# Prefix sums of a stick-breaking mixer in two rounded passes, value turns behind their slab, gate in PSUM, and fewer query columns

## What is computed

```python
z = einsum('bhqd,bhkd->bhqk', qb, kh) * scale
valid = key_pos < qpos
log_keep = where(valid, log_sigmoid(-z), 0.0)
after = cumsum(log_keep, axis=3, reverse=True) - log_keep
attn = where(valid, exp(log_sigmoid(z) + after), 0.0)      # then attn @ v, 8 heads of 64
u = a * sigmoid(b)                                         # GLU, then a causal conv of width 31 on 512 channels
```

## Time and profile before

| what | value |
|---|---|
| median of 3 runs | 1518.4 us (1518.07 to 1519.37) |
| profiled execution, its own time | 1519.34 us |
| its span in the profile | 1516.8 us |
| mean granted TensorE clock | 0.995 |
| PE busy | 1497.6 us (99%) |
| DVE busy | 1060.8 us (70%) |
| ACT busy | 757.5 us (50%) |
| POOL busy | 406.2 us (27%) |
| DMA | 250.90 MB, 165 GB/s mean |

### The profile page before, as it was taken

The page is one execution under the profiler, slowest core; times in us unless marked ns, Lnnn a source line. Parts: engine busy times, 40 slices in busy tenths (PEclk is TensorE's granted clock), DMA queues, the critical chain, the costliest instruction groups (busy, mean ns, idle before and its releaser), DMA issues.

```text
span 1516.8 us, 31248 instructions
## 1 busy us (share of the span) xinstructions
PE 1497.6 (99%) x11573; PEld 1447.4 (95%) x11573; DVE 1060.8 (70%) x1609; ACT 757.5 (50%) x1067; POOL 406.2 (27%) x162
## 2 busy tenths in 40 slices
PE   9999999999999999999999999999999999999997
PEld 7999999989999998999999999999998989999986
DVE  6438888758657778889765645755548998887854
ACT  6546655545444344457544544444444447644542
POOL 5542000533434300000244343434410000034452
PEclk9999999999999999999999999999999999999998
DMA  7334566655555544345555554556645335555662
GB/s 258 112 98 149 174 189 191 214 153 164 181 177 198 164 129 149 112 125 166 174 177 177 189 187 136 181 172 191 199 130 153 122 116 156 176 180 180 198 226 88
DMA packets 66119, 250.90 MB, mean 165 GB/s; under 512 B 7552, under 2 KB 8832, under 8 KB 66048
## 3 DMA queue, kind: packets, MB, share of 16 engines
q1 hardware_dynamic: 66048, 249.92, 52.6%
HBM read 248.84 MB, written 1.05 MB: 165 GB/s over the span
## 4 chain that ended last, share of the span: by engine, by line
PE 93%; DVE 5%; ACT 1%; issue 0%; DVEq 0%; ACTq 0%
PE W L1406 25%; PE W L1408 25%; PE W L1407 25%; PE W L1478 5%; PE XP L1502 4%; PE W L1477 3%; PE XQ L1502 2%; DVE scr L1265 2%; DVE wlo L825 1%; PE W L1446 1%; PE W L1447 1%; PE W L1448 1%; DVE proj L842 1%; PE XQ L1425 0%; ACT whi L428 0%
## 5 line engine op out<-in xcount | busy, mean ns | idle before, releaser
L1406 PE MATMUL W<-xh,whi 128*128 128x272 f32 (+2 forms) x2400 | 696.4, 290 | 1.6 <-DVE wlo L825 1.6
L381 POOL TENSOR_TENSOR wlo<-raw,whi 128x1024 fp32r<-128x1024 f32 (+1 forms) x151 | 403.6, 2674 | 1098.3 <-ACT whi L428 1098.3
L1408 PE MATMUL W<-xh,wlo 128*128 128x272 f32 (+2 forms) x2400 | 688.6, 287 | 0.0
L1407 PE MATMUL W<-xl,whi 128*128 128x272 f32 (+2 forms) x2400 | 686.8, 286 | 0.0
L428 ACT ACTIVATE whi<-raw 128x1024 fp32r<-128x1024 f32 (+1 forms) x437 | 482.0, 1109 | 143.6 <-PE W L1408 117.4
L1406 PEld LDWEIGHTS W<-xh,whi 128*128 128x128 f32 x2400 | 452.7, 189 | 7.1 <-issue 5.6
L1408 PEld LDWEIGHTS W<-xh,wlo 128*128 128x128 f32 x2400 | 453.0, 189 | 0.0
L1407 PEld LDWEIGHTS W<-xl,whi 128*128 128x128 f32 x2400 | 452.7, 189 | 0.3
L825 DVE TENSOR_TENSOR wlo<-raw,whi 128x1024 fp32r<-128x1024 f32 (+1 forms) x285 | 370.6, 1301 | 72.8 <-ACT whi L428 72.2
L1406 PE MATMUL W<-ax,whi 128*128 128x272 f32 (+2 forms) x816 | 235.1, 288 | 1.1 <-DVE ax L1239 0.5
L1408 PE MATMUL W<-ax,wlo 128*128 128x272 f32 (+2 forms) x816 | 234.3, 287 | 0.0
(11 more groups left out here) (235 smaller groups left out, 1202.4 us busy)
## 6 DMA issues: line engine op xcount, KB each, us to landing
raw<-in_w SPq DMA_DIRECT2D x357, 512.0 KB, 3.6
raw<-in_w SPq DMA_DIRECT2D x80, 704.0 KB, 4.1
h<-in_hT SPq DMA_DIRECT2D x4, 272.0 KB, 4.2
raw<-in_w SPq DMA_DIRECT2D x4, 256.0 KB, 4.6
out<-h SPq DMA_DIRECT2D x4, 256.0 KB, 2.5
scr<-in_cst SPq DMA_DIRECT2D x1, 1000.0 KB, 9.5
cst<-in_cst SPq DMA_DIRECT2D x1, 472.0 KB, 7.4
prm<-in_prm SPq DMA_DIRECT2D x1, 180.0 KB, 9.1
```

The lines of the kernel that those rows point to most:

```text
L381: pool.tensor_tensor(wlo[:, j, 0:cols], raw[:, j, 0:cols], whi[:, j, 0:cols].bitcast(F32), ALU.subtract).then_inc(lo_ready[j], 1)
L1406: pe.matmul(out, whi[:, j, w], mh, start=start and k == 0, stop=False, skip_group_check=True)
L1407: pe.matmul(out, whi[:, j, w], ml, start=False, stop=False, skip_group_check=True)
L1408: ins = pe.matmul(out, wlo[:, j, w], mh, start=False, stop=stop and k == len(rhs) - 1, skip_group_check=True)
```

## The change

- **Sums**: after `keeps`, ACT rounds `keep` into `keep_hi` (float32r), DVE takes the rest `keep_lo`, and `sums` runs its ten products twice, on `keep_hi` and on `keep_lo`, all in float32r, with weights in float32r that POOL copies once at the start (`minus_r`). ACT does its part in phase 2 ahead of `out_hi`, DVE its part first thing in phase 3.
- **Value turns**: the 12 turns follow slab 12 in one piece.
- **Low weights first**: for s < 8 DVE makes the low weights before it waits for the sigmoid and multiplies.
- **First block**: the query slabs of forgetting attention (4), of retention (2) and the four gate slabs are computed from token 14 on (258 columns for 272); POOL sets the query and key columns left out to zero. The silu goes head by head, three heads into PSUM, and each head's product waits for its own.
- **The end**: the last output chunk uses three products per block and one residual step; its square goes into the norm's product directly (`last_stat`), without the DVE sum.

```diff
@@ gpsimd, at the start
+            pool.tensor_copy(minus_r[:, :], cst[:, 2 * P:4 * P]).then_inc(hide_ready, 1)
...
+            pool.memset(proj[:, FQ:FK + 2 * CC - 1, 0:T_A], 0.0).then_inc(q_zero, 1)
@@ scalar
-            act.activation(proj[:, RG:RG + 4, :], proj[:, RG:RG + 4, :], ACT.Silu).then_inc(rg_ready, 1)
+            act.wait_ge(rn_step, 6)
+            for hd in range(RET_H):
+                act.activation(ret_silu(hd), proj[:, RG + hd, T_A:], ACT.Silu).then_inc(rg_ready, 1)
...
+                def keep_high(c):
+                    act.wait_ge(keep_ready, CC * l + c + 1)
+                    if c:
+                        act.wait_ge(cum_mm, CC * l + c)
+                    act.activation(keep_hi, keep, ACT.Copy).then_inc(half_keep, 1)
...
+                    if phase == 2 and 0 <= c < CC:
+                        keep_high(c)
@@ vector
+                def keep_rest(c):
+                    dve.wait_ge(half_keep, CC * l + c + 1)
+                    dve.tensor_tensor(keep_lo, keep, keep_hi.bitcast(F32), ALU.subtract).then_inc(keep_low, 1)
...
+                    if phase == 3 and 0 <= pair < CC:
+                        keep_rest(pair)
                     if phase == 3 and 1 <= pair <= CC:
                         out_lo(pair - 1)
...
-                        if s % 2:
-                            dve.wait_ge(glu_sig, CC * l + c + 1)
-                            dve.tensor_tensor(u[:, c, CONV_K - 1:], proj[:, c, :], proj[:, 4 + c, :],
-                                              ALU.mult).then_inc(u_ready, 1)
...
                     if s:
                         lo_ahead(g + s // 4, j, K8D, K8D)
+                    if s < G_GLU and s % 2:
+                        c = s // 2
+                        dve.wait_ge(glu_sig, CC * l + c + 1)
+                        dve.tensor_tensor(u[:, c, CONV_K - 1:], proj[:, c, :], proj[:, 4 + c, :],
+                                          ALU.mult).then_inc(u_ready, 1)
@@ tensor
+            def last_stat(p, t):
+                pe.wait_ge(acc_done, 8 * p + 7)
+                pe.matmul(X[3][:, t:T], ones, acc[:, t:], start=True, stop=False, skip_group_check=True)
+                pe.wait_ge(sq_ready, 8 * p + 8)
+                pe.matmul(X[3][:, t:T], ones, sq[:, 1, t:], start=False, stop=True, skip_group_check=True).then_inc(stat_mm, 1)
...
-                    pe.wait_ge(keep_ready, CC * l + c + 1)
+                    pe.wait_ge(keep_low, CC * l + c + 1)
...
+                    for part in (keep_hi, keep_lo):
+                        for bank in range(2):
+                            for b in range(3):
+                                w = T - P * b
+                                r = BLK[b][1] - BLK[b][0]
+                                mm(X[bank][:, SB_AT[b]:SB_AT[b] + w], minus_later[0:r, :], part[0:r, bank, SB_AT[b]:SB_AT[b] + w], False)
+                            mm(X[bank][:, P:T], minus_ones, part[:, bank, SB_AT[1]:SB_AT[2]], False)
...
-                            between=turn_v if s == G_V else None)
+                    if s == G_V:
+                        turn_v()
```

More of the change, by code:

```diff
@@ L211, in build @@
         prob_tail = s1("prob")[:, 0:T]
+        keep_hi, keep_lo = (ax[:, SPARE_KEEP + 2 * k:SPARE_KEEP + 2 * k + 2, :, :].rearrange("p c s t -> p (c s t)")[:, 0:2 * SBW]
+                            .rearrange("p (b n) -> p b n", b=2) for k in range(2))
         qz = s1("qz").rearrange("p (c n) -> p c n", c=CC)
@@ L295, in split_base, with first_token, ret_silu @@
             return DC * p
+        def first_token(s):
+            return T_A if s in range(FQ, FK + 2 * CC - 1, 2) or RQ <= s < RK or s >= RG else 0
+        def ret_silu(hd):
+            return (XQ[:, 0, T_A:T], XQ[:, 1, T_A:T], XP[:, 0, T_A:T], proj[:, RG + 3, T_A:])[hd]
         def ret_last(half):
@@ L873, in residual_tail @@
             def residual_tail(p, m, b, n, t):
-                dve.wait_ge(evac_done, n)
-                add_square(p, m, b, t)
-                if not (isinstance(p, int) and p in FINAL):
+                final = isinstance(p, int) and p in FINAL
+                if not (final and isinstance(m, int) and m == DC - 1):
+                    dve.wait_ge(evac_done, n)
+                    add_square(p, m, b, t)
+                if not final:
                     take_lo(p, m, t)
@@ L981, in group @@
                             dve.wait_ge(fin_h, m + 1)
-                        if j % 2 and t == T_B:
+                        if j % 2 and t == T_B and p in FINAL and isinstance(i, int) and j == 3:
+                            residual(p, DC - 1, j - 1, 4 * (g + i) + j + 1, 2, coef, t)
+                        elif j % 2 and t == T_B:
                             residual_halves(2 * i + j // 2, j - 1, 4 * (g + i) + j + 1, coef, 0 if g == G_DN1 else 1)
@@ L1223, in _ @@
                 else:
-                    scaled(proj[:, s, :], s % 4, s + 1).then_inc(evac_done, 1)
+                    if s == FQ:
+                        dve.wait_ge(q_zero, 1)
+                    t = first_token(s)
+                    scaled(proj[:, s, t:], s % 4, s + 1, t).then_inc(evac_done, 1)
                 if s == 2:
@@ L1479, in halves, with ffn_down, group @@
                 return ins
-            def ffn_down(g, f, t=0):
-                def group(i, first=False):
+            def ffn_down(g, f, t=0, final=False):
+                def group(i, first=False, last=False):
                     for j in range(4):
@@ L1486, in group @@
                             emptied(4 * (g + i) + j - 3)
-                        if t == T_B:
+                        if t == T_B and not (last and j >= 2):
                             halves(g + i, j, f, half, j - half, first and j < 2).then_inc(mm_done, 1)
@@ L1492, in ffn_down @@
                 group(0, first=True)
-                with pe.Fori(1, N_DN) as i:
+                with pe.Fori(1, N_DN - 1) as i:
                     group(i)
+                group(N_DN - 1, last=final)
             def out_proj(g, rhs, ready, behind=(3, 3, 3, 3), t=0):
@@ L1780, in sums @@
                 def sums(c):
-                    pe.wait_ge(keep_ready, CC * l + c + 1)
+                    pe.wait_ge(keep_low, CC * l + c + 1)
                     tail = T - 2 * P
[L1784 to L1792, removed]
+                    for part in (keep_hi, keep_lo):
[5 more added lines that the diff above has]
+                            mm(X[bank][:, P:T], minus_ones, part[:, bank, SB_AT[1]:SB_AT[2]], False)
+                            both = X[bank][:, P:SB_AT[2]].rearrange("p (s n) -> p s n", s=2)[:, :, P:P + tail]
+                            last = part[0:tail, bank, SB_AT[2]:SBW].rearrange("p (s n) -> p s n", s=1).to_broadcast([tail, 2, tail])
+                            ins = mm(both, minus_ones[0:tail, :], last, False)
                     ins.then_inc(cum_mm, 1)
@@ L1808, in values, with turn_v @@
                     ins.then_inc(o_mm, 1)
-                def turn_v(k):
-                    if k == 1:
-                        pe.wait_ge(evac_done, 4 * g + G_V)
-                    if k >= 1:
-                        for n in (2 * k - 2, 2 * k - 1):
-                            b, c = divmod(n, CC)
+                def turn_v():
+                    pe.wait_ge(evac_done, 4 * g + G_V)
+                    for b in range(3):
+                        for c in range(CC):
                             ins = turn(X[1 + b], c, proj[:, VV + c, :], b)
-                            if c == CC - 1:
-                                ins.then_inc(v2_mm, 1)
+                        ins.then_inc(v2_mm, 1)
                 def channel_sums(k):
```

38 lines of the change are left out of this document (20 added, 18 removed).

## The result

The changed kernel takes 1545.2 us (median of 4, 1539.9 to 1547.4) against 1518.9 for the one before beside it: a ratio of 1.016 (95% interval 1.013 to 1.019), 26 us slower. Predicted were 1522.7, in a range of 1513 to 1534: the sign is right, the size is not. The profiled execution took 1543.05 us, its span is 1541.2 us, 24.4 longer than that of before.

What follows compares the result with a forecast made beforehand. TensorE, busy 99% of the span, was taken as the bound. Terms -10.0 + 2.4 + 11.0 + 3.4 - 1.6 - 0.9 = +4.3 us, added to the median of 1518.4, gave 1522.7 us, range 1513 to 1534.

Steps and rivals of the forecast that it cites:

- The front: Start of each mixer, second block: turns behind slab 12 and low weights first save 5.0 us a layer, -10.0 us.
- The passes: The eight sums: two rounded passes take 4.2 to 4.3 us against 4.0, +0.3 us each, +2.4 us in all.
- four changes of weight height: In sums: one rounded pass of a bank streams 0.25 us but keeps all four height changes, 0.8 us, 1.05 us together.
- The first block: Fewer columns -1.4 us, late low weights on POOL +0.5 us, gate -0.7 us: sum -1.6 us.
- the gate: First block's gate: first two products take 2.10 us beside a POOL instruction; 0.7 us of 1.6 lost is regained.
- the end: Last output chunk: a residual step and the DVE sum go, PE's last slabs 0.1 us more; -0.9 us.
- The wait at c = 0: PE waits 2.2 us for DVE's keep_rest ahead of the first sums in both layers; part of the link's +11.0 us.
- the short ones: PE's waits for keep_rest at c > 0: 0.9 us in layer 0, 1.3 us in layer 1, three times each.
- I count one fall per layer: Clock drops to 0.50 behind the c = 0 wait in each layer, 1.7 us each, +3.4 us; bounds 0 and 13.6.
- The rival with a fall at each sum: Clock falls at all eight sums, 8 x 1.7 = 13.6 on 1519.3: 1532.9 us; chance 0.27.
- Many stretches at 0.50: Sign of being wrong; expected was clock 0.50 once per mixer, behind the first sums, and full behind slab 12.
- no row here shows a fall without a wait of 2 us: Remark on the earlier profile's rows, made against the rival in which the clock falls at each sum (chance 0.27).

## Why the prediction was wrong in size

**What held.** The front: 5.3 us a layer against 5.0. From the last product of slab 12 to that of slab 13, with the turns between, it is 582.49 - 577.39 = 5.1 us, the waits of the earlier trace rows are gone, and two runs undo the parts: turns behind the slab 7.0 us, low weights first 2.3. The 1.3 left of 10.6 is about the price of one fall of 3.4 us: the trace of before has one behind the turns' wait in each layer, the run with the turns inside in one only. The passes: 4.25 us a sum, within the 4.2 to 4.3; without a wait ahead 4.16 against 3.89, the predicted +0.3. The worked-out reason, four changes of weight height that each pass of a bank keeps, is confirmed by taking the changes out: 4.25 becomes 2.31. They are 1.9 of the 3.2 us that the prediction put between the products; the rest stays with 128 rows too. The first block, the gate and the end came within 0.1 us of their terms; they were read from the slabs' times only, not tried alone.

**What was off a little.** The wait at c = 0 is 2.09 for 2.2, the short ones 0.82 and 1.20 for 0.9 and 1.3. At the gate, were misread: the 2.10 us are of both products together, and only the first is long (1.74 us; the second takes 0.43). The gain there came to 0.6 us for the 0.7 taken.

**The step that failed** is, in its own words, "I count one fall per layer, 1.7 us each, +3.4 us; bounds 0 and, should each of the eight sums bring a fall, 13.6". Both factors were wrong. The number: eight falls, not two. The price: a fall was taken for 3.4 us at 0.50, as behind the wait of the earlier trace rows, but here a stretch goes on for up to 10.2 us, 6.0 on average, and the eight cost 20.2 us in 47.8, or 0.42 us for each us at half clock. So even the bound was 6.6 us too low. The rival with a fall at each sum, held at 0.27, named the right mechanism with that same price per fall: 1532.9, 12 us short. "Many stretches at 0.50" stood among the prediction's own signs of being wrong. Beside this term, the 4.5 us of the fall in the first block stood in no term at all; it comes and goes from one execution to the next.

**Why so many.** This table has the runs that vary the density of `sums` and the waits ahead of them (median; falls in the quads; us at half clock):

| sums | waits of 2.1, 0.8, 1.2 us | short or no waits |
|---|---|---|
| two rounded passes, 16-row products | 1545.2; 8; 47.8 | 1521.4; 7; 27.3 |
| one fp32 pass, 16-row products | 1529.3; 3; 27.3 | 1505.7; 0 |
| two rounded passes, 128 rows | 1509.6; 2; 10.2 | 1496.7; 0 |
| one rounded pass, 16-row products | not run | 1497.4; 1; 3.4 |
| one fp32 pass, 128 rows | not run | 1496.2; 0 |

A wait of 2 us can do it over fp32 sums, as the prediction had it from the earlier trace rows, and 4.2 us of thinly filled products can do it without a wait, which it had not: "no row here shows a fall without a wait of 2 us" was true of the trace, and was taken for more than it says. With both, the falls are more and longer. The prediction had even worked out the sign of it, 1.0 us of columns in the 4.3 us, and used it only to bring back one fall.

The Trainium skill, "TensorE: Matmul & The Clock Gate", section on psum-queue depth-cycling, has the clock swing where TensorE idles briefly and often. The short waits over fp32 sums agree with it once in six; the run without waits has seven falls with no idle time in the profile, which goes beyond it. The Trainium skill, "TensorE: Matmul & The Clock Gate", section on weight-path perf modes, says that 128 weights of a type other than FP32 load faster; the float32r loads of the 128-row run take 191 ns, like the 0.19 us of the fp32 ones in the earlier trace rows.

**Against the rounded passes as such**, with the falls set aside: rounding doubles the instructions (20 for 10, where each fp32 product leaves two records anyway), saves 1.0 us of columns and adds the link of 10 us. With 128 rows it saves 0.4 us a sum (2.31 for 2.71), 3.2 us in all, and costs the waits that are left of the link, 3.0 us: 1496.7 against 1496.2, no difference.

**Open.** Whether thin streaming brings the clock down or the changes of weight height do isn't told apart: 128 rows take both away, and a second rounded pass adds both. What sets the length of a fall (3.4, 6.8 or 10.2 us) isn't known. Each count above is of one profiled execution; the four of the changed kernel have mean clocks of 0.976 to 0.982 and times of 1539.9 to 1547.4, so the lengths differ from one to the next. So do those of the run with waits and fp32 sums (1524.1 to 1534.2, clocks 0.985 to 0.992): its three falls, and "five of six", are a sample. Why the clock falls in the first block in some executions only was not found; the one attempt at it, with the narrow products moved, didn't help.

## What to carry to other kernels

Before an fp32 product is split into rounded ones, count the products, the changes of weight height between them and the link that makes the parts, not the columns: here the columns halved and `sums` grew. Where a short block lies between full ones, give it all 128 rows if the rest is zero: that alone took 1.2 us of 3.9 off each sum, 9.6 us of the whole (1505.7 to 1496.2). With the front, the first block and the end of the change kept, the kernel is then 1.6% under the one before and 3.2% under the changed one. And read the granted clock behind every stretch in which little is streamed, also where PE is busy 100%; a fall seen once in the trace is no upper bound for the next.

## What the runs showed of the hardware that was not expected

- The granted clock fell to 0.50 without any idle time of TensorE in the profile: seven times behind 4.2 us of narrow float32r products, and in the first block behind 3.4 us in which PE and its loads were busy (3.40 and 3.15 us).
- One fall costs 1.5 us (3.4 us at 0.50, in the value turns) to 4.5 us (10.2 us, in the first block); the stretches at 0.50 lasted 3.4, 6.8 or 10.2 us.
- The same program falls or doesn't: times of 1495.9 to 1496.6 and of 1500.1 to 1500.7 for one kernel, 10.2 us at half clock between them.
- A product with 16 rows of weights between products with 128 is dearer than one with 128 rows: ten fp32 products take 3.89 us with four short ones and 2.71 with none; twenty rounded ones 4.25 and 2.31.
- A wait as long as 2.1 us does not always bring a fall: in the value turns (turns inside, one fp32 pass) it did in one layer of two, and with rounded sums of 128 rows in one of two as well.
